# Hymba decoder layer in float32: the block products of the second down projection without GpSimd, in a new order, with the first activations read back in the eighth round

## The reference, cut to what matters

```python
def swiglu(x, w_gate, w_up, w_down):
    return (jax.nn.silu(x @ w_gate) * (x @ w_up)) @ w_down

x = x + 0.5 * rmsnorm(swiglu(rmsnorm(x, g1), ...), g2)                   # ffn1
x = x + rmsnorm(hybrid_mixer(rmsnorm(x, g3), cos, sin, ...), g4)
x = x + 0.5 * rmsnorm(swiglu(rmsnorm(x, g5), w_gate, w_up, w_down), g6)  # ffn2
```

## Time and profile before

| | us |
|---|---|
| median of three runs | 2277.1 |
| the profiled execution | 2276.56 |
| its span, from first to last instruction | 2274.8 |
| PE busy in the span | 2209.6 |
| DVE busy | 1741.1 |
| POOL busy | 350.4 |

### The profile page before, as it was taken

How to read it: one execution, slowest core, us unless ns; L and a number is a source line. 1 busy time by engine, 2 the same in 40 slices (tenths; PEclk the granted TensorE clock), 3 DMA queues, 4 the chain that set the end, 5 groups by cost and what they waited for, 6 DMA issues and landing times.

```text
span 2274.8 us, 29629 instructions
## 1 busy us (share of the span) xinstructions
PE 2209.6 (97%) x10304; PEld 1809.2 (80%) x10304; DVE 1741.1 (77%) x2550; ACT 965.1 (42%) x1725; POOL 350.4 (15%) x290
## 2 busy tenths in 40 slices
PE   9999999999999999999999999999899999989989
PEld 7888888888877877778788777788788888868867
DVE  8877777777759777786666676878877777789997
ACT  6322222222334576787531674224422323335443
POOL 0000000000000344444100225100000000033572
PEclk9999999999999999999999999999999999999999
DMA  4111111111323001001121234132122222285734
GB/s 161 54 53 43 54 55 55 55 40 47 117 98 125 20 10 38 29 18 57 59 82 47 75 119 174 60 100 105 53 87 83 83 83 83 83 312 201 231 116 148
DMA packets 78179, 199.83 MB, mean 88 GB/s; under 512 B 8448, under 2 KB 10496, under 8 KB 76288
## 3 DMA queue, kind: packets, MB, share of 16 engines
q1 hardware_dynamic: 78080, 198.56, 26.0%
HBM read 165.69 MB, written 32.83 MB: 87 GB/s over the span
## 4 chain that ended last, share of the span: by engine, by line
PE 84%; DVE 7%; ACT 3%; issue 3%; POOL 2%; DMA 1%; SPq 0%; DVEq 0%; ACTq 0%; POOLq 0%
PE psum L473 11%; PE psum L474 11%; PE psum L475 11%; PE psum L641 4%; PE psum L643 4%; PE psum L642 4%; PE psum L2437 3%; PE psum L2439 3%; PE psum L2438 3%; PE psum L1517 3%; PE psum L1519 3%; PE psum L1518 3%; PE psum L2583 2%; PE psum L2980 1%; PE psum L2594 1%
## 5 line engine op out<-in xcount | busy, mean ns | idle before, releaser
L1476 POOL TENSOR_TENSOR down_w_raw<-down_w_raw,down_w_two 128x512 f32<-128x512 f32 x55 | 88.0, 1611 | 665.0 <-DMA down_w_two<-in_d 664.9
L770 ACT CAST t_hi<-t_raw 128x512 fp32r<-128x512 f32 x152 | 93.6, 621 | 204.4 <-DVE t_raw L991 151.3
L1190 DVE TENSOR_TENSOR acc<-psum,acc 128x512 f32<-128x512 f32 x144 | 98.9, 691 | 80.5 <-PE psum L643 79.1
L792 ACT ACTIVATE sum<-sum 128x512 f32<-128x512 f32 x76 | 48.1, 633 | 231.7 <-DVE sum L1130 139.7
L1517 PE MATMUL psum<-down_b_hi,down_w_hi 128*128 128x512 f32 x308 | 123.0, 400 | 8.9 <-DVE down_w_lo L1508 8.9
L2437 PE MATMUL psum<-norm_hi,tile_hi 128*128 128x512 f32 x320 | 129.1, 403 | 1.9 <-DVE z_scaled L2845 1.9
L2754 DVE TENSOR_TENSOR probs_t_lo<-psum,probs_t_hi 128x512 fp32r<-128x512 f32 x144 | 97.1, 685 | 39.8 <-ACT probs_t_hi L2671 38.9
L473 PE MATMUL psum<-norm_hi,plain_hi 128*128 128x512 f32 x304 | 119.2, 392 | 7.5 <-DVE up_lo L1013 7.5
L2439 PE MATMUL psum<-norm_hi,tile_lo 128*128 128x512 f32 x320 | 125.0, 391 | 0.0
L2438 PE MATMUL psum<-norm_lo,tile_hi 128*128 128x512 f32 x320 | 124.8, 390 | 0.0
L766 ACT CAST plain_hi<-up_raw 128x512 fp32r<-128x512 f32 x76 | 47.1, 619 | 180.7 <-DMA up_raw<-in_gu 177.9
(11 more groups left out here) (456 smaller groups left out, 6477.9 us busy)
## 6 DMA issues: line engine op xcount, KB each, us to landing
down_w_raw<-in_d SPq DMA_DIRECT2D x77, 256.0 KB, 2.9
gate_raw<-in_gu SPq DMA_DIRECT2D x38, 512.0 KB, 4.3
up_raw<-in_gu SPq DMA_DIRECT2D x76, 256.0 KB, 3.9
raw_tile<-in_w_att SPq DMA_DIRECT2D x28, 512.0 KB, 3.6
down_w_two<-in_d SPq DMA_DIRECT2D x55, 256.0 KB, 4.4
act_scratch<-act_stage SPq DMA_DIRECT2D x21, 512.0 KB, 5.2
tile_lo_raw<-in_d SPq DMA_DIRECT2D x20, 512.0 KB, 4.2
x_scratch<-acc SPq DMA_DIRECT2D x32, 256.0 KB, 2.0
```

The costliest lines, as they stand in the source:

```text
L770: act.copy(to, of).then_inc(sem(p + "_t_hi"), 1)
L1190: v.tensor_tensor(x, banks(4 + d % 4), x, ALU.add).then_inc(sem(p + "_acc"), 1)
```

## The change

1. `POOL_B` and its semaphore are gone, and GpSimd does nothing in the block products. DVE does all 55 `w_sum` and all 55 `b_sum`. The first three `w_sum` of product 0 are written into the last loop tile's code.
2. `end_plan` has other costs and ranks, `cols` and `rows` get a k-step of product 5 behind which they stand at the earliest, and the last third of the second rows (`late_in`) and `b_in` are issued later, behind the loads of (1, 3) and (1, 6).
3. The first 11 rows of activations (`act_first_rows`, three DMAs) are read back in the hardware loop, after its tile (7, 1), and no longer after `w_in` (0, 1) at the end.
4. Slot 9 of the ring is (152, 60) KB and no longer (152, 156), where 156 is the stage of the last activations. The waits of SP and ACT for the last store fall away for k = 9.
5. The difference of the token halves has a buffer of its own in the turn, `x_difference_turn`. It waits for the second half of x alone and not for a round of matmuls. Ranks of the turn change with it.

The core of the diff:

```diff
-              (214.75, 218.75), (152, 156), (180, 184))
+              (214.75, 218.75), (152, 60), (180, 184))
-POOL_B = (5, 6)
...
+                rounds(2, FIRST_ROWS)
+                down_first_rows_sp(sp)
+                rounds(FIRST_ROWS, LAST_PAIR)
...
             def difference():
-                wait(v, p + "_gu_mm", 2 if t == "t0" else 3)
-                v.tensor_tensor(d3[:], acc[:, 0:KH, half(0)], acc[:, 0:KH, half(1)], ALU.subtract).then_inc(sem(p + "_s_dve"), 1)
+                if t == "t0":
+                    wait(v, p + "_gu_mm", 2)
+                else:
+                    v.wait_ge(sem("half_x"), past_half("t2", 1, KT) + KT)
+                v.tensor_tensor((d3 if t == "t0" else d3_turn)[:], acc[:, 0:KH, half(0)], acc[:, 0:KH, half(1)], ALU.subtract).then_inc(sem(p + "_s_dve"), 1)
...
+                elif not more:
+                    down_w_sum(v, 0, 0)
+                    down_w_sum(v, 0, 1)
...
                 elif p == "f2":
+                    down_w_sum(v, 0, 2)
                     for k in range(2):
                         down_b_lo(v, 0, k)
                         down_w_lo(v, 0, k)
...
-            if m == 0 and k == 9:
-                sp.wait_ge(sem("act_out"), 16 * FT)
-            elif m == 0 and k == 10:
+            if m == 0 and k == 10:
...
+        def down_first_rows_sp(sp):
+            sp.wait_ge(sem("act_out"), 16 * (2 * FIRST_ROWS - 1))
+            sp.wait_ge(sem("half_out"), 16 * past_half("t3", 0, KT))
+            wait(sp, "f2_s_dve", 13)
+            for g in range(3):
+                down_rows_in(sp, 0, slice(0, S), g, f"dn_b_first{g}")
...
-            down_w_in(sp, 0, 7)
-            down_w_in(sp, 0, 8)
+            for k in range(7, 10):
+                down_w_in(sp, 0, k)
             store(LAST_PAIR, 1)
             down_w_in(sp, 0, 10)
-            down_w_in(sp, 0, 9)
+
+        def down_late_in(sp):
+            sp.wait_ge(sem("act_out"), 16 * FT)
             down_rows_in(sp, 1, half(1), 2, "dn_b_second2")
...
+            def settled(e):
+                plan.steps[("cols", e)][2].append(("mm", 5, 7))
+                plan.steps[("rows", e)][2].append(("mm", 5, 9))
...
-                            add("POOL", "w", ("w_sum", m, k), 1.45, w)
+                            add("DVE", "w_sum", ("w_sum", m, k), 0.61, w)
...
-            rank |= {("DVE", "add"): 1, ("ACT", "put"): 1, ("DVE", "w"): 2, ("DVE", "b"): 2, ("DVE", "b_sum"): 2, ("ACT", "w"): 2,
-                     ("ACT", "b"): 2, ("DVE", "a_sum"): 3, ("DVE", "resid"): 4, ("DVE", "scale"): 5, ("POOL", "w"): 2,
-                     ("POOL", "b_sum"): 2, ("SP", "w_in"): 1}
+            rank |= {("DVE", "add"): 0, ("ACT", "put"): 0, ("DVE", "w"): 2, ("DVE", "b"): 2, ("DVE", "b_sum"): 3, ("DVE", "w_sum"): 3,
+                     ("ACT", "w"): 2, ("ACT", "b"): 2, ("ACT", "a_sq"): 1, ("DVE", "a_sum"): 1, ("DVE", "resid"): 4,
+                     ("DVE", "scale"): 5, ("SP", "w_in"): 1}
...
-            sums += [(2.2, [("round", 2, KT - 1)])] + [(0.69, [("difference_hi", k)]) for k in range(KH)]
+            sums += [(2.2, [("resid", "t2", 1, KT - 1)])] + [(0.69, [("difference_hi", k)]) for k in range(KH)]
...
-                     ("ACT", "t_hi"): 7, ("DVE", "sums"): 6, ("DVE", "t_sum"): 6, ("DVE", "t_lo"): 7}
+                     ("ACT", "t_hi"): 1, ("DVE", "sums"): 6, ("DVE", "t_sum"): 1, ("DVE", "t_lo"): 0}
```

More of the change, by code:

```diff
@@ L801, in tile @@
                     wait(act, p + "_read", at_tile(i, s, 11, 8 - 11))
+                    if isinstance(i, int) and i == 1 and not s:
+                        wait(act, p + "_prod", 4)
                     act.copy(e1[:], banks(0)).then_inc(sem(p + "_s_out"), 1)
@@ L1399, in b_sums @@
         def b_sums(m, k):
-            same = [n for n in range(m) if len(DOWN_B[n]) > 1 and (n in POOL_B) == (m in POOL_B)]
-            return FG * len(same) + k + 1
+            return FG * sum(len(x) > 1 for x in DOWN_B[:m]) + k + 1
         def puts_to(m, d):
@@ L1972, in turn_plan @@
             for k in range(KH):
-                add("ACT", "s", ("difference_hi", k), 0.63, ("planned_sum", 12))
+                add("ACT", "s", ("difference_hi", k), 0.63, ("planned_sum", 12), ("round", 0, KT - 1))
             for n in range(2):
@@ L1977, in turn_plan @@
             for n in range(4):
-                add("DVE", "t_sum", ("operand_sum", n), 0.69, ("seven_in",), ("planned_sum", 16),
+                add("DVE", "t_sum", ("operand_sum", n), 0.69, ("seven_in",),
                     ("operand_sum", n - 1) if n else None)
@@ L3423, in _ @@
                     down_w_lo(v, *e)
+                elif step == "w_sum":
+                    down_w_sum(v, *e)
                 elif step == "b_sum":
```

69 lines of the change are left out of this document (30 added, 39 removed).

## The result

The changed kernel took 2253.05 us in the median of four runs (2251.45 to 2254.22), the kernel before 2277.26 beside it (2274.57 to 2277.59). The ratio is 0.9896 with a 95% interval of 0.9879 to 0.9913: 1% faster. 2249.5 had been forecast, with a range of 2243 to 2263; of the 27.6 us that were to be gained 24.2 came.

What follows compares the result with a forecast made beforehand. TensorE was taken as the bound, busy 2209.6 of 2274.8 us, so gains come from its idle time and slow-clock matmuls. 2276.56 - 5.4 - 9.4 - 13.1 + 0.5 = 2249.2, predicted as 2249.5; range 2243 to 2263.

Steps and rivals of the forecast that it cites:

- A: Turn to the seven-product tiles: PE's wait and slow matmuls cost 9.8 us, 4.4 would stay, gain 5.4 (3.5 to 7).
- B: Start of the block products, product 0: 12.7 us lost, 3.3 would stay, gain 9.4 (5 to 12).
- C: Product 5, where PE waits for the norm: 13.1 us of stall, all to go; lower bound 8.
- The 0.60 for each VectorE instruction: Block products: without GpSimd's SBUF reads each 128x512 VectorE operation, old or new, costs 0.60 us.
- Rival 3: Block products: VectorE becomes the bound, its slowness being its own and not GpSimd's; slower, 2317 us; chance 0.04.
- The clock term: Product 0, behind the wait at the fourth k-step: matmuls at the lower clock lose 0.5 us.
- The first activations, +0.5: Hardware loop: early row loads delay gate_raw, costing PE 0 to 3.4 us, taken as 0.5.
- The clause that the early loads help the start: Start of the block products: an earlier store and w_in there, counted within B's gain of 9.4 us.
- The tail, 0: Behind the last block product: the tail takes 12.7 us and keeps its chain; change 0, between -1 and +1.
- Does VectorE keep up?: Products 0 to 6: VectorE needs 196 us against PE's 209, so no new waits; priced at nothing.
- Rivals 1 and 4: 1: A, B, C gain only lower ends, 2260.6, chance 0.14; 4: B, C stalls return behind loads, 2273, 0.03.
- rival 2: Hardware loop: first rows make gate_raw and up_raw 4.1 us late, slow matmuls follow; 2254 us; chance 0.04.

Runs made afterwards that it cites:

- rows_late: Changed kernel with the three loads of the first activations back at their old place at the end; 2246.73 us, ratio 0.9866 to the kernel before.
- rows_split: Changed kernel with its three early first-activation loads issued apart, behind tiles (6, 1), (7, 1) and (8, 1); 2250.33 us, ratio 0.9883 to the kernel before.
- sums_alone: Kernel before the change with VectorE forming all sums of the block products, planner ranks and the rest old; 2284.35 us, ratio 1.0035.

## Why the prediction was right, and where it was off

The bound, the three places and the sign were as read from the earlier trace rows. That the total came so near is in part luck, as the misses of its terms went both ways: by the pieces A gave 1.3 more than forecast, B and C 1.2 and 1.3 less, the loop lost 1.4 more and the tail 0.9, and 1.8 of the span's 25.1 come from a stretch ahead of the change. By its steps:

- **The 0.60 for each VectorE instruction.** Right. Lows at 685, sums at 687, 199.5 us of VectorE's work in the block products against 196 forecast. Rival 3 fell, and the two kernels with idle GpSimd work show the cause: an instruction of GpSimd that reads SBUF beside VectorE's with two SBUF operands (804 against 685 and 678). The Trainium skill says the same in SBUF — State Buffer, "Who interferes with whom"; it also says that a GpSimd instruction that only writes does not contend, and the memsets agree (685).
- **A, the turn, -5.4.** 4.8 shorter as a pause, and 1.9 of slow matmuls less in this execution: -6.7. The wait was forecast at 2.7 and is 2.64, and `up` ends it as in the walk; its 1.5 of slow clock did not come here. It came in two of the nine profiled executions with the same pause of 3.03.
- **B, the start, -9.4.** It gave 8.2. Both waits are as walked (0.60 for 0.7, 1.86 for 2.1), and VectorE's row has the eight lows between them:

```profile
2024.04 0.68 DVE L1489 TENSOR_TENSOR down_w_raw<-down_w_raw,down_w_two 128x512 f32<-128x512 f32 x1
2024.64 4.91 DVE L1524 TENSOR_TENSOR down_b_lo<-act_first_rows,down_b_hi 128x512 fp32r<-128x512 f32 x8
2029.45 0.69 DVE L1519 TENSOR_TENSOR down_w_lo<-down_w_raw,down_w_hi 128x512 fp32r<-128x512 f32 x1
```

  The clock term was set at 0.5 and cost 1.6 in this execution, none in the other.
- **C, product 5, -13.1.** It gave 11.8. No wait at `cols`, as forecast. Missing in the sum was what follows from the place of `rows` behind k-step 10: product 6 waits 0.77 for ACT's copy of them. The norm's matmuls cost 1.9 and not 1.4, which is what is left over 29.92 where `rows` stand a k-step earlier (31.8) and nothing waits.
- **The first activations, +0.5.** The term that was sized worst: it cost 1.9, and slow matmuls on top in some executions. The issue of gate_raw, its use, and the rows' landing:

```profile
1910.17 0.36 SPq L388 DMA_DIRECT2D gate_raw<-in_gu  x1
...
1916.98 0.69 DVE L1001 TENSOR_TENSOR t_raw<-gate_raw 128x512 f32<-128x512 f32 x1 [4.23 <-DMA gate_raw<-in_gu]
```

```profile
DMA to landing us min/median/max: 9.4/14.3/18.0
```

  The three are issued from 1896.6 to 1897.6 and the last lands 18.0 later, near 1915.6; gate_raw, issued at 1910.17, is used at 1916.98, 6.8 later and not 4.5, and PE waits 1.7, a pause of 2.1 between starts, with seven or eight slow matmuls in three of the seven executions that have this pause. What happened lies between the two cases of the prediction: gate_raw landed neither 4.5 behind the rows nor as if they weren't there, but 1.3 behind them, and was 2.3 late. VectorE's wait of 4.23 is over the 3 that had been set as a sign. The clause that the early loads help the start is refuted by rows_late: the two waits of PE are the same without them. This part of the change costs 2.3 to 4.2 us (the loop's piece in the two executions of the changed kernel against rows_split) and brings nothing.
- **The tail, 0.** It took 0.9 more, at the edge of what was allowed for, and the chain did not stay: before, residual transposes followed the last block matmul at once; now the first transposes are those of `down_sums`, which wait 0.78 for VectorE's last add, and the last residual load is issued 2.9 ahead of the last block matmul's end and not 8.1.
- **Does VectorE keep up?** Yes, but the condition that the prediction gave for it is not enough. I argued with totals, 196 against 209. In sums_alone the total is the same and PE stood 14.2 for six sums at the wrong place. The planner's ranks carry the gain as much as the engine that does the sums: the sums alone gave +8, the sums with the ranks -6, everything but the sums -1, all but the turn -19, the whole -22 to -24.

Rivals 1 and 4 fell, as A, B and C gave 6.7, 8.2 and 11.8 against lower ends of 3.5, 5 and 8; of rival 2 a part came, 1.9 us of waiting in the loop and in some executions slow matmuls behind it.

Left open: why the same pause is followed by slow matmuls only at times, and the 6 us between the medians of rows_late and the changed kernel, of which the loop's pause and its slow matmuls account for 2.3 to 4.2. The stretch ahead of the last plain matmul took from 1630.0 to 1638.4 in the fourteen profiled executions, which is more than such a rest; that it explains it is not shown.
